# Last layer norm of a two-layer decoder step: block 3 by VectorE from PSUM, the sample rows' arithmetic on GpSimd, block 3 stored ahead of block 2

## The reference, cut to what matters

```
def layer_norm(x, g, b):
    mu = jnp.mean(xf, axis=-1, keepdims=True)
    var = jnp.mean(jnp.square(xf - mu), axis=-1, keepdims=True)
    y = (xf - mu) * lax.rsqrt(var + LN_EPS) * g + b
```

## Time and profile before

| what | us |
|---|---|
| median of 3 runs (lowest, highest) | 1412.6 (1409.61, 1415.02) |
| the profiled execution | 1411.87 |
| its span, first to last instruction | 1410.2 |
| start of the last transposes of blocks 2 and 3 | 1396.36 |
| last DVE operation ends | 1407.0 |
| last store issued | 1407.38 |

### The profile page before, as it was taken

One profiled execution on the slowest core, in us unless ns is written; L12 is line 12 of the kernel. 1 busy time (PEld: TensorE's weight loads), 2 busy tenths in 40 slices (PEclk: granted clock), 3 DMA queues, 4 the chain that ended last, 5 costly groups with the idle time before them and its releaser, 6 DMA issues. The chain is left out here.

```text
span 1410.2 us, 27562 instructions
## 1 busy us (share of the span) xinstructions
PE 1352.2 (96%) x11310; PEld 1287.1 (91%) x11310; DVE 728.9 (52%) x1390; ACT 506.1 (36%) x1014; POOL 395.1 (28%) x467
## 2 busy tenths in 40 slices
PE   6999997999999999999899999999999999999996
PEld 5999995999999999999899866668999999999996
DVE  3423975486333343344889756454764343343435
ACT  3322224454223133132642366686444132230311
POOL 3014433563011010016644472024652010110102
PEclk9999999999999999999999899999999999999998
DMA  5252252032222313121432235204303313232201
GB/s 158 98 143 71 79 157 88 5 120 81 100 95 86 109 72 121 60 68 46 86 89 39 66 109 188 62 4 118 105 17 120 120 61 119 69 112 84 97 31 62
DMA packets 87101, 123.87 MB, mean 88 GB/s; under 512 B 24338, under 2 KB 42206, under 8 KB 86944
## 3 DMA queue, kind: packets, MB, share of 16 engines
q1 hardware_dynamic: 82048, 107.00, 23.6%
q0 software_dynamic: 4928, 15.10, 3.5%
HBM read 115.62 MB, written 8.57 MB: 88 GB/s over the span
## 5 line engine op out<-in xcount | busy, mean ns | idle before, releaser
L1063 PE MATMUL ps<-xh,ring_lo 128*128 128x260 f32 (+2 forms) x2496 | 505.6, 284 | 4.3 <-issue 2.2
L1063 PEld LDWEIGHTS ps<-xh,ring_lo 128*128 128x128 f32 (+2 forms) x2496 | 384.3, 188 | 6.2 <-ACT big L1679 2.7
L1063 PE MATMUL ps<-xl,wr 128*128 128x260 f32 x1568 | 351.3, 283 | 6.0 <-DVE xl L2177 3.6
L1063 PE MATMUL ps<-xh,wr 128*128 128x260 f32 x1568 | 353.0, 284 | 1.4 <-DVE ring_lo L2079 1.0
L1063 PEld LDWEIGHTS ps<-xl,wr 128*128 128x128 f32 x1568 | 255.3, 188 | 8.0 <-DVE xl L2177 5.0
L1063 PEld LDWEIGHTS ps<-xh,wr 128*128 128x128 f32 x1568 | 255.9, 188 | 3.5 <-ACT att L1716 1.4
L866 POOL TENSOR_TENSOR att<-att 128x520 f32<-128x520 f32 (+1 forms) x80 | 77.4, 969 | 548.5 <-DVE att L2103 521.4
L2079 DVE TENSOR_TENSOR ring_lo<-ring,wr 128x1024 fp32r<-128x1024 f32 (+1 forms) x144 | 192.3, 1338 | 70.5 <-ACT wr L1679 70.3
L1063 PE MATMUL ps<-hh,wr 128*128 128x260 f32 x1024 | 222.1, 283 | 0.0
L1063 PE MATMUL ps<-hh,ring_lo 128*128 128x260 f32 x1024 | 221.8, 283 | 0.0
L1063 PE MATMUL ps<-hl,wr 128*128 128x260 f32 x1024 | 221.7, 283 | 0.0
(11 more groups left out here) (356 smaller groups left out, 1584.2 us busy)
## 6 DMA issues: line engine op xcount, KB each, us to landing
ring<-in_w_up SPq DMA_DIRECT2D x16, 2048.0 KB, 7.9
ring<-in_w_down SPq DMA_DIRECT2D x16, 2048.0 KB, 8.0
ring<-in_w_in_e SPq DMA_DIRECT2D x9, 1024.0 KB, 5.8
ring<-in_w_in_e SPq DMA_DIRECT2D x2, 2048.0 KB, 8.5
ring<-in_w_out_e SPq DMA_DIRECT2D x2, 2048.0 KB, 8.4
ring<-in_w_in_o SPq DMA_DIRECT2D x16, 256.0 KB, 4.9
ring<-in_cache_kv POOLq DMA_DIRECT2D x32, 128.0 KB, 2.4
ring<-in_w_out_o SPq DMA_DIRECT2D x8, 512.0 KB, 7.8
```

The lines of the kernel that those rows point to most:

```text
L1063: last = pe.matmul(bank(g, half)[0:width(g), 0:H2], w[:, k, :], x[:, k, cols(half)], start=first, stop=final)
```

## The change

Block 3 is no longer standardised by ACT. DVE reads it from PSUM, subtracts the mean and multiplies by the gain in one operation a half, and in a second operation a half multiplies by the reciprocal of the deviation and adds the bias. Of the sample rows DVE keeps the sums and the reciprocal; ACT copies the means out of PSUM, and POOL does the variance and the four operations on `xsm`, ahead of its shift of block 2. SP stores block 3 ahead of block 2. DVE's gain of block 2 is now its last work, behind the whole of block 3 and the reciprocal for the sample rows. The semaphore counts follow.

```diff
@@ SP
-            for i in range(QT):
+            for i in (0, 1, 3, 2):
                 for q in range(2):
                     sp.wait_ge(sm["y_a" if i < 3 else "y_b"], 2 * i + q + 1 if i < 3 else q + 1)
...
-            sp.wait_ge(sm["smp_a"], 2)
+            sp.wait_ge(sm["smp_a"], 3)
@@ POOL
-            for i in range(3):
+            def shifted(i, at):
+
                 for q in range(2):
-                    pool.wait_ge(sm["yg_ok"], 2 * i + q + 1)
+                    pool.wait_ge(sm["yg_ok"], at + q + 1)
                     y = ytm[:, i, 512 * q:512 * q + 512]
                     pool.tensor_tensor(y, y, bB[:, 512 * q:512 * q + 512], ALU.add).then_inc(sm["y_a"], 1)
+
+            shifted(0, 0)
+            shifted(1, 2)
+            pool.wait_ge(sm["smp_a"], 1)
+            link(pool.tensor_tensor(svar, smean[:, 0:B], smean[:, 0:B], ALU.mult))
+            link(pool.tensor_tensor(svar, smean[:, B:2 * B], svar, ALU.subtract))
+            pool.tensor_scalar(svar, svar, 0.0, LN_EPS, ALU.max, ALU.add).then_inc(sm["smp_v"], 1)
+            link(pool.tensor_tensor(xsm, xsm, smean[:, 0:B].unsqueeze(1).to_broadcast([P, KD, B]), ALU.subtract))
+            pool.wait_ge(sm["smp_v"], 3)
+            link(pool.tensor_tensor(xsm, xsm, svar.unsqueeze(1).to_broadcast([P, KD, B]), ALU.mult))
+            link(pool.tensor_tensor(xsm, xsm, colT[:, 3 * KD:4 * KD].unsqueeze(2).to_broadcast([P, KD, B]), ALU.mult))
+            pool.tensor_tensor(sout.rearrange("p (b k) -> p k b", k=KD), xsm,
+                               colT[:, 32 + 3 * KD:32 + 4 * KD].unsqueeze(2).to_broadcast([P, KD, B]),
+                               ALU.add).then_inc(sm["smp_v"], 1)
+            shifted(2, 6)
@@ PE
-            pe.wait_ge(sm["smp_v"], 3)
+            pe.wait_ge(sm["smp_v"], 4)
             tr(ps[5][0:KD * B, 0:P], sout, P).then_inc(sm["y_mm"], 1)
@@ ACT
+            act.wait_ge(sm["y_mm"], 2 * QT + 1)
+            copy(smean, ps[4][:, 0:2 * B]).then_inc(sm["smp_a"], 1)
             spread(2)
             spread(3)
             standard(2)
             act.wait_ge(sm["smp_v"], 2)
             act.activation(svar, svar, ACT.Sqrt).then_inc(sm["smp_a"], 1)
-            standard(3)
@@ DVE
-                for i in (2, 3):
-                    block_scale(i)
-                dve.wait_ge(sm["y_mm"], 2 * QT + 1)
-                link(dve.tensor_copy(smean, ps[4][:, 0:2 * B]))
-                link(dve.tensor_tensor(svar, smean[:, 0:B], smean[:, 0:B], ALU.mult))
-                link(dve.tensor_tensor(svar, smean[:, B:2 * B], svar, ALU.subtract))
-                dve.tensor_scalar(svar, svar, 0.0, LN_EPS, ALU.max, ALU.add).then_inc(sm["smp_v"], 1)
+                block_scale(2)
+                for q in range(2):
+                    dve.scalar_tensor_tensor(ytm[:, 3, 512 * q:512 * q + 512], y_bank(3, q)[:, :], bmv[3][:, 0:1],
+                                             gB[:, 512 * q:512 * q + 512], ALU.subtract, ALU.mult).then_inc(sm["yg_ok"], 1)
+                dve.wait_ge(sm["ys_ok"], 4)
+                link(dve.reciprocal(bsd[3], bsd[3]))
+                for q in range(2):
+                    y = ytm[:, 3, 512 * q:512 * q + 512]
+                    dve.wait_ge(sm["yg_ok"], 5 + q)
+                    dve.scalar_tensor_tensor(y, y, bsd[3], bB[:, 512 * q:512 * q + 512], ALU.mult, ALU.add).then_inc(sm["y_b"], 1)
+                dve.wait_ge(sm["smp_a"], 2)
+                dve.reciprocal(svar, svar).then_inc(sm["smp_v"], 1)
                 block_gain(2)
-                dve.wait_ge(sm["smp_a"], 1)
-                link(dve.reciprocal(svar, svar))
-                link(dve.tensor_tensor(xsm, xsm, smean[:, 0:B].unsqueeze(1).to_broadcast([P, KD, B]), ALU.subtract))
-                link(dve.tensor_tensor(xsm, xsm, svar.unsqueeze(1).to_broadcast([P, KD, B]), ALU.mult))
-                link(dve.tensor_tensor(xsm, xsm, colT[:, 3 * KD:4 * KD].unsqueeze(2).to_broadcast([P, KD, B]), ALU.mult))
...
-                block_gain(3)
-                block_shift(3)
```

More of the change, by code:

```diff
@@ L2225, in last_norm @@
                     block_stats(i, 1)
-                for i in (2, 3):
-                    block_scale(i)
-                dve.wait_ge(sm["y_mm"], 2 * QT + 1)
-                link(dve.tensor_copy(smean, ps[4][:, 0:2 * B]))
-                link(dve.tensor_tensor(svar, smean[:, 0:B], smean[:, 0:B], ALU.mult))
-                link(dve.tensor_tensor(svar, smean[:, B:2 * B], svar, ALU.subtract))
-                dve.tensor_scalar(svar, svar, 0.0, LN_EPS, ALU.max, ALU.add).then_inc(sm["smp_v"], 1)
-                block_gain(2)
-                dve.wait_ge(sm["smp_a"], 1)
-                link(dve.reciprocal(svar, svar))
-                link(dve.tensor_tensor(xsm, xsm, smean[:, 0:B].unsqueeze(1).to_broadcast([P, KD, B]), ALU.subtract))
-                link(dve.tensor_tensor(xsm, xsm, svar.unsqueeze(1).to_broadcast([P, KD, B]), ALU.mult))
-                link(dve.tensor_tensor(xsm, xsm, colT[:, 3 * KD:4 * KD].unsqueeze(2).to_broadcast([P, KD, B]), ALU.mult))
-                dve.tensor_tensor(sout.rearrange("p (b k) -> p k b", k=KD), xsm,
-                                  colT[:, 32 + 3 * KD:32 + 4 * KD].unsqueeze(2).to_broadcast([P, KD, B]),
-                                  ALU.add).then_inc(sm["smp_v"], 1)
-                block_gain(3)
-                block_shift(3)
+                block_scale(2)
[10 more added lines that the diff above has]
+                dve.reciprocal(svar, svar).then_inc(sm["smp_v"], 1)
+                block_gain(2)
             def block_stats(i, q):
@@ L2263, in block_gain @@
                     dve.tensor_tensor(y, y, gB[:, 512 * q:512 * q + 512], ALU.mult).then_inc(sm["yg_ok"], 1)
[L2265 to L2269, removed]
             def xe_low(k):
```

## The result

| | before | changed |
|---|---|---|
| median of 22 runs (lowest, highest), us | 1412.7 (1407.46, 1415.47) | 1415.86 (1412.63, 1420.0) |
| ratio, 95% interval | | 1.0021 [1.0012, 1.0030] |
| profiled execution, span, us | 1411.87, 1410.2 | 1412.63, 1411.0 |

The changed kernel is slower by 0.21%, 3.0 us (interval 1.7 to 4.2 us); I had forecast 0.0. Its time lies in my range, but the interval excludes no change.

The account below looks back on a forecast made before the run. It took DVE's chain up to the last prompt store as the bound: DVE 3.4 us earlier (-6.25, +2.84), all taken back by POOL's 4.6 us chain, net 0.0 us, so 1412.6 us; range 1408.5 to 1416.7 us.

Parts of the forecast that it names:

- The step that failed: End of the program: last half of the last prompt block ready, plus a fixed 3.2 us (1407.0 to 1410.2).
- with 3 us to spare: POOL's shift of block 2 in the kernel before: ended at 1403.96, 3 us before it was wanted.
- Block 3 ready at T+5.2: DVE's tail: block 3 finished at 1402.22, 4.7 us earlier than before.
- A step of DVE's new operation at 0.66 us: DVE's four new 128x512 operations on block 3: 0.66 us a step, bounds 0.60 and 0.78.
- DVE 3.4 us earlier: End of DVE's work: 6.25 us removed, 2.84 us added, so done 3.4 us earlier.
- The means' copy on ACT hidden: ACT ahead of block 2's root: a 0.20 us copy ending near 1397.8, hidden in idle time, 0.3 us of room.
- Small operations on POOL: POOL's sample-row work: 0.33 us for 64 elements, 0.22 us for 8.
- The turns of DVE and POOL: Tail: operations with two SBUF inputs on DVE and POOL take turns, so POOL's shifts end at 1406.96.
- The dear sample operations: Second rival, POOL's three sample-row operations: 0.73 us each, with slow DVE steps 1.7 us later, 1414.3 us; chance 0.15.
- First use of `tensor_scalar` on POOL: Third rival, POOL's variance: dear first use delays all that follows, at twice the room 3 us, 1415.6 us; chance 0.04.
- Delivers what DVE loses: Fourth rival, the tail: the kernel gains DVE's whole 3.4 us, 1409.2 us; chance 0.02.
- the first rival: POOL's sample operations and DVE's gain do not delay each other: 0.8 us less, with low bounds 1411.5 us; chance 0.15.

Follow-up runs that it names:

- the change put right: The changed kernel with POOL's sample-row work done early and block 2's bias added by DVE instead of POOL; ratio to before 0.9974 [0.9957, 0.9992].
- the small programs: Not the kernel: one tile loaded, one DVE and one POOL addition, one store; POOL's closing drain 1364 ns, with 64 POOL DMAs added 6617 ns.

## Why the prediction was wrong

**The step that failed** is in its first part: "the end is 'the last half of the last prompt block is ready' plus a fixed 3.2 us". It took the 2.8 us behind the last store as the store's own. They were 2.3 us of store and 0.5 us of waiting for POOL's drain. From this followed the second error, that POOL's shift of block 2 had ended "with 3 us to spare". It had nothing to spare: with the drain behind it, it was already what ended the program. The change moves it from T+6.92 to T+9.53, 2.61 us, and the tail grows by 2.55.

**The steps that held.** Block 3 ready at T+5.2 (T+5.17 measured). A step of DVE's new operation at 0.66 us: two take 1.32 us to the start of what follows with the PSUM source and 1.34 with the SBUF source, alike. DVE 3.4 us earlier (measured 3.4). The reciprocal at T+5.3. The means' copy on ACT hidden (T+0.48 to T+0.66, the root of block 2 at T+1.06 as before). Small operations on POOL at 0.20 us for 8 elements (0.22 forecast) and 0.30 for 64 (0.33). The turns of DVE and POOL: L1023 and L1024 took 0.58 and 0.62 us under DVE's two gains and L1025 0.30 behind them, and the second gain was the longer one, 0.81 us. The experiments that took one partner away confirm it: 0.22 us for DVE's small operations with POOL silent, about 0.3 for POOL's without a DVE operation of two SBUF inputs beside them. The shift ended 0.4 us earlier than the sum said, nearly all of it in the three operations on the sample rows (1.66 us with their gaps instead of 2.03). So the sum for the last prompt store was right within 0.4 us, and it was the wrong thing to sum. That the time still fell into my range is luck of a wide range: no case in it stood for this wait.

**The rivals.** The dear sample operations did not occur: 0.58, 0.62 and 0.30 us, the first two of them held up by DVE, against 0.73 for the rival. First use of `tensor_scalar` on POOL: 0.25 us, nothing dear about it. "Delivers what DVE loses", 3.4 us, comes near to what the change put right does: a tail 2.8 us shorter than before, once POOL is out of it. I had excluded that only for this order of POOL's queue, and rightly. Two slips of the text: the sum without turns is the shorter one of the first rival, not of the second, and the third rival's 1415.6 is 3.0 us above my case, not 2.8. What I had no rival for is an end of the program that is set by an engine whose last record lies 6 us earlier.

The Trainium skill, "VectorE: DVE Perf Modes", section "The DRAIN you can't avoid", says that DRAINs of the preamble and postamble take about 12 ns, constant, on all five engines. The rows here stand at a line of the kernel, so they need not be the ones that it means. Whoever takes its number for them goes wrong: SP's 7 ns come near it, and ACT's and PE's 8 ns in the small programs, but in the full kernel ACT's takes 301 ns, PE's 477 and POOL's 5950.

## What to carry to other kernels

Before you say what ends a program, read the rows of its last line, where the engines meet, and ask for each engine when its closing drain ends, not when its last operation does. POOL has a long one here when it has issued many DMAs (90 DMAs, 6 us), so take it out of the tail first; giving it fewer DMAs should shorten the drain, but no run took any away from this kernel. SP issues most of the loads and all stores of the last norm, and its drain takes 7 ns. POOL's work may be moved to the engine that looks busiest, if that one is waiting for POOL anyway. And compare tails from a common event in the trace, not by span: here the event itself moved by 9 us from profile to profile, while the last store of the kernel before and of the two that add only something late on POOL was issued 10.33 to 10.35 us behind it in all three.

## What the runs showed that I had not expected

POOL's closing drain takes 66 to 94 ns for each DMA that POOL has issued since the start, though all had landed: 0.09 us more for 1, 5.25 us more for 64, 1.37 us more for 16 on top of 90; and nothing for 400 more operations. It starts when POOL's queue is at its end, even if POOL has only waited. That DVE gains 1.8 us from POOL's absence and loses only 1.2 by doing POOL's work was in the rows of before, and I had used it only against the change.
